# Two-block transformer stack on one core: moving TensorE's operands to other byte offsets

## The reference

```python
def first_block(...):              # 2 layers, x and ctx: 512 rows, of which layer 2 drops 256 midway
    for layer in range(2):
        h = h + 0.5 * g1 * swiglu(prenorm(h), ffn1_w_in, ffn1_w_out)    # hidden 2816
        mix = even_mixer(...) if layer == 0 else odd_mixer(...)         # Fourier + gated linear attention /
        h = h + gm * (mix @ mix_w_out)                                  # short conv + differential attention
        h = h + 0.5 * g2 * swiglu(prenorm(h), ffn2_w_in, ffn2_w_out)
    return rmsnorm(h)

def second_block(x, ...):          # 2 layers, 256 rows
    for i in range(2):
        mix = retention(...) if i == 0 else dilated_attention(...)
        x = layer_norm(ALPHA * x + mix)
        x = layer_norm(ALPHA * x + swiglu(x, w_up, w_down))             # hidden 2816
    return x
```

## Time and profile before

| what | value |
|---|---|
| runs | 2685.91, 2686.26, 2691.38 us, median 2686.26 |
| the profiled execution: its span | 2685.8 us |
| TensorE matmul busy | 2627.7 us, 98% |
| TensorE weight load busy | 2324.4 us, 87% |
| VectorE busy | 1484.3 us, 55% |
| ScalarE busy | 1042.3 us, 39% |
| GpSimd busy | 199.0 us, 7% |
| DMA, share of 16 engines (q1) | 46.5% |
| mean granted clock of TensorE | 0.993 |

### The profile page before, as it was taken

One profiled execution on the slowest core, in us unless ns is written; L12 is line 12 of the kernel. 1 busy time (PEld: TensorE's weight loads), 2 busy tenths in 40 slices (PEclk: granted clock), 3 DMA queues, 4 the chain that ended last, 5 costly groups with the idle time before them and its releaser, 6 DMA issues.

```text
span 2685.8 us, 40437 instructions
## 1 busy us (share of the span) xinstructions
PE 2627.7 (98%) x17444; PEld 2324.4 (87%) x17444; DVE 1484.3 (55%) x1985; ACT 1042.3 (39%) x1402; POOL 199.0 (7%) x192
## 2 busy tenths in 40 slices
PE   6999999989999999999999999999999999999998
PEld 4788888878888888888887899999999999988998
DVE  4666654746565556553364665565555554565554
ACT  3322223634212223222243554443754454455443
POOL 0000000111000010000011000010010020144001
PEclk9999999999999999999999999999999999999999
DMA  7544445115435344353262275554445466663452
GB/s 254 179 159 156 154 152 169 48 60 173 141 118 180 130 153 157 133 164 99 70 198 71 72 232 192 158 194 155 158 160 177 159 202 189 189 151 102 160 196 85
DMA packets 376080, 405.98 MB, mean 151 GB/s; under 512 B 7264, under 2 KB 352176, under 8 KB 375904
## 3 DMA queue, kind: packets, MB, share of 16 engines
q1 hardware_dynamic: 375904, 403.40, 46.5%
HBM read 402.25 MB, written 1.12 MB: 150 GB/s over the span
## 4 chain that ended last, share of the span: by engine, by line
PE 92%; DVE 3%; ACT 2%; issue 2%; POOL 1%; DMA 0%; SPq 0%; DVEq 0%; POOLq 0%; ACTq 0%
PE bank L97 91%; PE bank L100 1%; DVE w_lo L108 1%; ACT w_hi L104 1%; POOL acc L108 1%; DVE tmp L116 0%; DVE df_sc L125 0%; DMA ident<-in_ident 0%; ACT df_e L105 0%; ACT x_hi L104 0%; DVE hT L116 0%; ACT at_pT L104 0%; ACT L104 0%; DVE acc L108 0%; DMA lim<-in_limits 0%
## 5 line engine op out<-in xcount | busy, mean ns | idle before, releaser
L108 DVE TENSOR_TENSOR w_lo<-w_raw,w_hi 128x2048 fp32r<-128x2048 f32 (+2 forms) x331 | 698.0, 2112 | 765.6 <-ACT w_hi L104 765.1
L97 PE MATMUL bank<-x_hi,w_hi 128*128 128x256 f32 (+1 forms) x3000 | 988.9, 330 | 4.3 <-DVE x_lo L116 2.2
L97 PE MATMUL bank<-x_hi,w_lo 128*128 128x256 f32 (+1 forms) x3000 | 979.2, 327 | 0.0
L97 PE MATMUL bank<-x_lo,w_hi 128*128 128x256 f32 (+1 forms) x3000 | 974.1, 326 | 0.0
L104 ACT ACTIVATE w_hi<-w_raw 128x2048 fp32r<-128x2048 f32 (+2 forms) x331 | 577.9, 1750 | 383.2 <-PE bank L97 232.4
L97 PEld LDWEIGHTS bank<-x_hi,w_hi 128*128 128x128 f32 x3000 | 572.7, 191 | 65.9 <-issue 17.0
L97 PEld LDWEIGHTS bank<-x_hi,w_lo 128*128 128x128 f32 x3000 | 572.6, 191 | 47.4
L97 PEld LDWEIGHTS bank<-x_lo,w_hi 128*128 128x128 f32 x3000 | 570.3, 191 | 46.7 <-issue 0.7
L97 PE MATMUL bank<-hid_hi,w_hi 128*128 128x512 f32 (+1 forms) x1056 | 357.1, 338 | 0.0
L97 PE MATMUL bank<-hid_hi,w_lo 128*128 128x512 f32 (+1 forms) x1056 | 355.5, 337 | 0.0
L97 PE MATMUL bank<-hid_lo,w_hi 128*128 128x512 f32 (+1 forms) x1056 | 355.4, 337 | 0.0
(11 more groups left out here) (276 smaller groups left out, 2336.3 us busy)
## 6 DMA issues: line engine op xcount, KB each, us to landing
w_raw<-in_ffn_w_in SPq DMA_DIRECT2D x88, 1024.0 KB, 5.9
w_raw<-in_ada_w SPq DMA_DIRECT2D x72, 1024.0 KB, 8.0
w_raw<-in_ffn_w_up SPq DMA_DIRECT2D x44, 1024.0 KB, 5.1
w_raw<-in_attn_w_in SPq DMA_DIRECT2D x36, 1024.0 KB, 5.3
w_raw<-in_ffn_w_out SPq DMA_DIRECT2D x32, 768.0 KB, 4.7
w_raw<-in_ret_w_in SPq DMA_DIRECT2D x24, 1024.0 KB, 5.3
w_raw<-in_ffn_w_out SPq DMA_DIRECT2D x32, 640.0 KB, 4.2
w_raw<-in_odd_w_in SPq DMA_DIRECT2D x12, 1024.0 KB, 5.4
```

What stands on the lines that cost most here:

```text
L97: return Issued(self.eng and self.eng.matmul(out, lhsT, rhs, start=start, stop=stop, skip_group_check=loose))
L108: return Issued(self.eng and self.eng.tensor_tensor(out, a, b, op))
```

## The change

The tensor `lead`, 24 float32 a partition (96 bytes), is allocated ahead of w_raw and never used, so w_raw, w_hi, w_lo and the whole working area move up by 96 bytes. hid_hi, hid_lo and the two `sums` buffers, in the working area, move up by another 128.

```diff
 XN, MID, TEMPS, WORK = 0, 32768, 90496, 106880
 UNIT = 2048
 NRAW, NSPLIT = 4, 3
+LEAD, HID_AT = 24, 128

 def hidden(k, tag):
-    return Operand(tag, k.place("hid_hi", MID, [P, 12, 2 * T], F32R), k.place("hid_lo", MID + 24576, [P, 12, 2 * T], F32R))
+    at = MID + HID_AT
+    return Operand(tag, k.place("hid_hi", at, [P, 12, 2 * T], F32R), k.place("hid_lo", at + 24576, [P, 12, 2 * T], F32R))

         k.diag, k.lam = sb("diag", [P, 4, P]), sb("lam", [P, 8])
+        sb("lead", [P, LEAD])
         k.raw = sb("w_raw", [P, NRAW, UNIT])

-        k.sums = [k.place(f"sums{i}", MID + 49152 + 4096 * i, [P, 2, 512]) for i in range(2)]
+        k.sums = [k.place(f"sums{i}", MID + HID_AT + 49152 + 4096 * i, [P, 2, 512]) for i in range(2)]
```

## The result

| | runs | median us | lowest to highest |
|---|---|---|---|
| before | 18 | 2686.86 | 2684.41 to 2691.38 |
| changed | 18 | 2694.18 | 2690.40 to 2695.73 |

The changed kernel takes 1.0024 times as long (95% interval 1.0018 to 1.003), 7.3 us more. The forecast was 16 us less. The profiled execution took 2691.63 us and spans 2689.8.

A forecast was written before the change was run, and what follows sets the result against it. TensorE, busy 98%, was taken as the bound, through spacing between matmul starts. 14,760 products at 1.1 ns less each gave 16 us off 2,686.3, so 2,670 us; range 2,540 to 2,700.

The forecast's parts named there:

- What bounds the kernel: Whole span: TensorE busy 98%, so time is the spacing of matmul starts, 226.7 ns at 512 columns, 120.0 at 256.
- 14,760 products x 1.1 ns = 16 us less: All split-operand products: each gains 1.1 ns from its new place, giving 2,670 us; this small gain had chance 0.31.
- odd: Second layer's mixer: products with odd_hi 64 bytes off the weights, at 118.9 ns against 120.0, taken as place's effect.
- relation (a): All 14,760 split products: operands' absolute place modulo 256 changes from 160 to 0, hid's to 128.
- relation (b): Distance from moving operand to weights modulo 256: stays 0 for 11,592 products, becomes 128 for hid's 3,168.
- the slower one: Rival on hid products: distance 128 hurts, 120 to 126 ns for half or all, 2,696 or 2,705 us; chance 0.18.
- No change: Rival: the fixed cost belongs to loading 128 weights, whatever the place; 2,686 us; chance 0.29.
- the fixed 13.3 ns: Every split product, both widths: time beyond its columns at 2.4 GHz, 197 us in all, all the change can touch.
- The whole piece goes: Rival: runs starting 32 bytes into a 128-byte block touch one extra; fixing it gives 2,548 us; chance 0.22.
- The lower bound of 112: 256-column products: spacing cannot go under 112 ns, the closest full-size load and matmul pair, df_v,df_aT; gain at most 8.
- The waits for w_lo: PE waiting for split weights: costed at nothing, worth at most 1.5 us if the cover of weight transfers went.
- The rule of 16-byte lines: Skill text on SBUF reads: 160 and 0 touch the same number of lines, so the sum would be zero.

The follow-up runs named there:

- lead_only: Against the changed kernel, hid's extra 128 bytes removed, only the 96 bytes of lead kept: 2688.27 us against 2687.82 for the kernel before, ratio 1.0000.
- scan4: Against the kernel before, hid_hi and hid_lo at different distances from the weights, pairs of 0 with 64, 128 or 192 bytes, at each width: 2693.34 us, one run.
- apart192: Against the kernel before, the whole working area 192 bytes further from the weights: 2687.25 us, one run.
- best: Against the kernel before, movable 256-column operands (hid, rt, at, second-block x, first block's last feed-forward x) 192 bytes further from the weights: 2645.67 us, ratio 0.9845.
- scan2: Against the changed kernel, lead out and hid at 256, 288, 320, 352, 384 or 192 bytes from the weights by feed-forward half: 2690.75 us, one run.
- own_next: Against the kernel before, 128 bytes put between w_hi and w_lo, hid in two layouts, to test which weights the distance is to: 2711.11 us, one run.
- best2: Against best, the first 128-row chunk of x2_hi and x5_hi put back at distance 0 from the weights: 2645.01 us, ratio 0.9837 to the kernel before.

## Why the prediction was wrong

**What bounds the kernel** was right. The time is the distance between starts of matmuls: waits grew by 1.2 us, and the change of the time is the count of hid products times the change of their spacing.

**The step that failed** is the sum, "14,760 products x 1.1 ns = 16 us less". It took odd's average gain as what place, relation (a), does for every product. Relation (a) is worth 0 (lead_only, 1.0000 with x and hid at 226.7 and 120.0). Odd gains by the 64 bytes between its parts, which the change leaves as they were: its 118.8 stayed when both parts moved by 96 bytes, and hid laid out like it in scan4 shows 118.9. What the change does alter, the distance of hid (relation (b)), the sum left out: it costs 9.3 us at 512 columns and gives 2.1 at 256, 7.2 us more. The text had named both readings of odd and priced only one for the forecast. The sign to look for, "if only hid moves, relation (b) is what counts", is what came.

**The rival that came true** is the slower one: the distance of 128 hurts hid. Its threshold was a mean of 1.7 ns a hid product; measured is (5.9 − 1.3) / 2 = 2.3. Its size was off, 10 to 19 us for 7: it took 6 ns, from a long step of odd, for both widths. That is right at 512 columns (5.7 to 6.7) and has the wrong sign at 256 (−1.3), so the near fit at 512 is partly luck: the 6 ns came from a single step of a 256-column product. Nothing in the trace of before shows a 512-column product at a distance other than 0, so its cost couldn't be read there.

**No change** was half right: for x, and so for 11,592 products, the fixed 13.3 ns stayed whatever the place. Its claim that nothing has odd's kind of distance after the change missed hid.

**The whole piece goes** is refuted: at place 0, the start of a block of 128 bytes, x is at 226.70 and 120.00. That 13.3 ns is the time of 32 columns proved no block of 128 bytes; the steady spacings all fit steps of 6.67 ns (below), and 13.3 is two of them. Yet the piece can shrink: 113.33 is half of it gone at 256 columns. The lower bound of 112, from the closest float32 pair, wasn't passed by the mean of any stage.

**The waits for w_lo** were costed at 1.5 us if cover went. They were 1.6 in the changed kernel and became 2.7 at most in any run (apart192; 2.6 in best, with PE 41 us faster). So they played no part, though the bound itself was 1 us too low.

**The rule of 16-byte lines.** The Trainium skill, "Advanced Engine Details and Errata", section SBUF Cachelines, has SBUF read in lines of 16 bytes, and gave zero for a move from 160 to 0. For that move the runs agree (1.0000). It says nothing of the distance between operands: multiples of 16 gave anything from 226.7 to 236.7 ns at 512 columns and from 113.3 to 120.0 at 256. Starts off those lines, 4 and 8 bytes, gave 237.97 and 233.34.

**What stays open** is the mechanism. The spacing depends on the distance modulo 256 (scan2), isn't a sum of each product's own cost (own_next, scan4), and at 192 two rhythms keep themselves up at the same addresses (apart192, best, best2), as 128 has two at 512 columns. What picks one isn't shown: the spacing changes only at a pause, and hid at 192 always got 113.33 when it was entered from products at distance 0, but best2 has a stretch that began so and didn't. That weight loads and streams settle into a phase would fit the sequences that repeat exactly; that is argued, and no run shows it.

## What to carry to other kernels

Where a matmul-bound kernel loads weights for each product, read the start-to-start distance stage by stage, and put the moving operand's distance to the weights modulo 256 bytes among the things to tune: here 0 for 512 columns and 192 for 256, worth 41 us of 2,687, while a shift of everything together (160 to 0) is worth nothing. Give each stage's tensor a distance of its own in one scan kernel, and confirm a good value over several stretches before using it, since one can be lucky. An anomaly in one group of a trace (odd) has as many explanations as it has differences from its neighbours; price each of them before one carries the sum.

## What the runs showed of the hardware

The uneven ones repeat a sequence, and the whole sequence is again a number of steps: 117.78 is 53 steps over three products, 118.67 (distance 128) is 89 over five, 232.38 is 244 over seven, 228.9 (64) is 103 over three, 234.29 (160) is 246 over seven, 118.9 (odd's layout in scan4) is 107 over six. Nearly all steady stretches fit; 237.97 (4 bytes) repeats nothing that I can find.
- A rhythm is kept over hundreds of products and across tensors: in apart192, 113.33 over the 1,438 last products of the last feed-forward and 117.78 over as many in the first one of 256 columns, with the same addresses.
- A distance is good for one width and bad for the other: 192 costs 6.7 ns at 512 columns and gives 6.7 at 256, or 2.2 in its slower rhythm.
- Runs of one kernel differ by up to 5.6 us, and much of it goes with the clock: of 38 runs of the kernel before, the eight with a mean granted clock of 0.994 or more took 2684.55 to 2686.05 us, and the nine with 0.992 took 2687.67 to 2689.86.
